# A new written order for the steps of the first kind of layer, on TensorE, ScalarE and VectorE

## The reference

```python
z = rms_norm(x, pre_mix_g) @ w_in            # 3256 columns, cut into 18 parts
o_A = chunk_gla(silu(q) * 64 ** -0.5, k, i, log_f)      # "A", hgrn2: 4 heads of 64
o_B = chunk_gla(q * 32 ** -0.5, k, v, log_gk)           # "B", gla: 4 heads, keys of 32
#   S_t = diag(f_t) S_{t-1} + k_t v_t^T ; o_t = S_t^T q_t
o_C = mla_attention(q_nope, q_rope, k_nope, k_rope, v)  # "C", causal softmax attention
o_D = chunk_gated_delta(qd, kd, vd, beta, log_g)        # "D", gated delta rule, 4 chunks of 64
x = x + rms_norm(concat(o_A, o_B, o_C, o_D) @ w_out, post_mix_g)
# then a gated feed-forward with a causal convolution
```

## Time and profile before

| | before |
|---|---|
| median of 3 runs | 1624.33 us (1623.91 to 1624.46) |
| the profiled execution | 1623.88 us, its span 1621.8 us |
| PE busy | 1538.5 us, 95% of the span |
| DVE busy | 1111.7 us, 69% |
| ACT busy | 811.2 us, 50% |
| mean granted TensorE clock | 0.973 of full |
| mixer of layer 0, first to last matmul | 27.8 to 229.7 us |
| mixer of layer 1 | 443.5 to 647.0 us |

### The profile page before, as it was taken

The page is one execution under the profiler, slowest core; times in us unless marked ns, Lnnn a source line. Parts: engine busy times, 40 slices in busy tenths (PEclk is TensorE's granted clock), DMA queues, the critical chain, the costliest instruction groups (busy, mean ns, idle before and its releaser), DMA issues.

```text
span 1621.8 us, 26707 instructions
## 1 busy us (share of the span) xinstructions
PE 1538.5 (95%) x10572; PEld 1319.4 (81%) x10572; DVE 1111.7 (69%) x1623; ACT 811.2 (50%) x1303; POOL 20.8 (1%) x36
## 2 busy tenths in 40 slices
PE   7998979999999989899999899899999889899998
PEld 7997668888898856788889787788879778788886
DVE  3866677885476666688855887876454798777545
ACT  3533265664435334566544546655355346655334
POOL 0010100000001010000000000000000000000000
PEclk9999889999999989899999899999999999999999
DMA  7431035565553211556563332555545343456552
GB/s 254 152 118 60 24 104 169 167 214 197 168 169 101 80 30 61 183 167 215 188 190 114 113 103 96 175 189 195 198 165 164 104 105 104 130 184 201 199 182 104
DMA packets 185275, 236.62 MB, mean 146 GB/s; under 512 B 24480, under 2 KB 155328, under 8 KB 185024
## 3 DMA queue, kind: packets, MB, share of 16 engines
q1 hardware_dynamic: 182080, 230.18, 44.0%
q0 software_dynamic: 3072, 4.74, 1.1%
HBM read 232.78 MB, written 2.10 MB: 145 GB/s over the span
## 4 chain that ended last, share of the span: by engine, by line
PE 77%; DVE 8%; issue 6%; ACT 3%; DMA 2%; DVEq 2%; ACTq 1%; POOL 0%; SPq 0%; POOLq 0%
PE banks L440 76%; DVE all_ring_rounded L2814 2%; DMA all_ring<-in_w_in 1%; DMA all_ring<-in_w_ple_gate 1%; ACT all_ring_rounded L2632 1%; DVE all_rest L2983 1%; DVE all_work L2918 1%; DVE all_work L2880 1%; DVEq L2917 0%; POOL all_work L2093 0%; PE banks L2299 0%; DVE all_work L2902 0%; DVE all_work L2876 0%; PE banks L955 0%; ACT all_work L351 0%
## 5 line engine op out<-in xcount | busy, mean ns | idle before, releaser
L440 PE MATMUL banks<-all_work_rounded,all_ring_rounded 128*128 128x512 f32 (+2 forms) x4160 | 650.2, 318 | 13.3 <-DVEq L436 10.3
L440 PEld LDWEIGHTS banks<-all_work_rounded,all_ring_rounded 128*128 128x128 f32 (+1 forms) x4160 | 584.8, 190 | 76.6 <-DVEq L436 12.0
L440 PE MATMUL banks<-all_ring_rounded,all_work_rounded 128*128 128x512 f32 (+2 forms) x2304 | 501.8, 378 | 13.5 <-DVE all_ring_rounded L2814 10.4
L440 PEld LDWEIGHTS banks<-all_ring_rounded,all_work_rounded 128*128 128x128 f32 x2304 | 410.1, 192 | 95.9 <-DVE all_ring_rounded L2814 16.1
L2814 DVE TENSOR_TENSOR all_ring_rounded<-all_ring,all_ring_rounded 128x2048 fp32r<-128x2048 f32 x104 | 237.8, 2292 | 119.7 <-ACT all_ring_rounded L2632 117.4
L1641 DVE TENSOR_TENSOR all_ring_rounded<-all_ring,all_ring_rounded 128x2048 fp32r<-128x2048 f32 (+2 forms) x96 | 213.9, 2233 | 72.2 <-ACT all_ring_rounded L1388 70.5
L2632 ACT ACTIVATE all_ring_rounded<-all_ring 128x2048 fp32r<-128x2048 f32 x104 | 198.6, 1912 | 121.2 <-DMA all_ring<-in_w_mlp_down 86.8
L1388 ACT ACTIVATE all_ring_rounded<-all_ring 128x2048 fp32r<-128x2048 f32 (+2 forms) x96 | 177.8, 1859 | 103.3 <-DMA all_ring<-in_w_in 43.4
L440 PE MATMUL banks<-all_work 64*64 64x64 f32 (+8 forms) x2180 | 156.4, 272 | 23.5 <-ACT all_work L2636 9.1
L440 PEld LDWEIGHTS banks<-all_work 64*64 64x64 f32 (+5 forms) x2180 | 114.8, 153 | 58.6 <-issue 24.1
L440 PE MATMUL banks<-all_work,all_ring 128*128 128x128 f32 x704 | 102.1, 289 | 2.4 <-DVEq L409 1.9
(11 more groups left out here) (264 smaller groups left out, 1206.7 us busy)
## 6 DMA issues: line engine op xcount, KB each, us to landing
all_ring<-in_w_in SPq DMA_DIRECT2D x48, 1024.0 KB, 5.4
all_ring<-in_w_mlp_up SPq DMA_DIRECT2D x32, 1024.0 KB, 5.3
all_ring<-in_w_mlp_down SPq DMA_DIRECT2D x32, 1024.0 KB, 4.8
all_ring<-in_ffn_w_gate SPq DMA_DIRECT2D x22, 1024.0 KB, 5.4
all_ring<-in_ffn_w_up SPq DMA_DIRECT2D x22, 1024.0 KB, 5.6
all_ring<-in_ffn_w_down SPq DMA_DIRECT2D x22, 1024.0 KB, 4.9
all_ring<-in_w_out SPq DMA_DIRECT2D x16, 512.0 KB, 4.4
all_ring<-in_w_out SPq DMA_DIRECT2D x8, 1024.0 KB, 5.0
```

The source lines that it names most:

```text
L440: ins = self.nc.tensor.matmul(out, lhsT, rhs, start=start, stop=stop)
```

## The change

Only the three texts of ORDER change, for PE, ACT and DVE. `name:n` means n steps of that part in a row. The set of steps is the same for each engine, but for their order. `panel` and `mix` on PE are empty steps.

```diff
         "PE": in_order("""
-            panel in:3 panel:2 in:3 panel in:8 panel:2 D in:2 panel D panel in:2 A:2 D in panel A D A D A in:3 D panel D
-            A D A panel in panel D A D in panel A D in A D in panel D A D A in A D A in A D:2 panel B D A B D A D mix B
-            D C B D C B D B panel B:3 D:2 B D C D B C B D B C B:2 early D B early C early B early C:2 rest C:2 rest C
-            late mix rest:2 late"""),
+            in:16 D:3 in D in D:2 in A:3 in A D:2 A in A in A D A D A D in A D A in D in A D A in D in D B:2 D A:2 D
+            A:2 D B in D B D B D B C:3 B D B D B D B D B D C B D:2 B C B:2 early B:2 early C:2 early:2 C rest C:2 rest
+            late C rest:2 late panel:16 mix:2"""),
         "ACT": in_order("""
-            panel:4 in panel in:7 panel in:7 D panel in:2 D panel in panel A in D A D in:2 A panel D A:2 D A panel D in
-            D A in D A D in panel:2 A:2 D in D:2 panel D A in:2 A:3 D A D:3 A B mix panel in A D B D:2 B D panel D C B C
-            D B D B:3 D B C B D C B D:2 C B:5 C:2 rest early rest early C rest late rest C late C early C early mix"""),
+            panel:2 in:5 panel:2 in:2 panel in D in:2 D in:2 panel in:2 panel in:2 panel D:2 in:5 A:2 D:2 panel A
+            panel A:2 D:2 A:2 in D:2 A:2 in:2 D:2 A:3 D:2 panel:2 in:2 A:3 panel D:2 in:2 panel D:2 B:2 A:2 D:9 B:2 C
+            B panel:2 B C:2 B:6 C:3 D:2 B:5 C:5 rest:4 early:4 late:2 mix:2"""),
         "DVE": in_order("""
-            in:2 panel:3 in h:2 in:3 panel:2 in panel in:2 D in:7 panel:2 in D in panel in D A:2 D A D:2 in A in A D in
-            A panel D A panel in D in A D panel A D panel in A D:2 in A:2 D:2 in panel A:4 D in panel D B D A D B D:2 B
-            mix B C D C panel B:2 D B:2 D B D:2 B C D B:3 D C B D B C early B:2 mix C early C:4 early late rest:2 C
-            rest:2 late early"""),
+            h in:2 panel:2 in:2 panel h panel in:2 panel in:2 panel in D:2 in:6 D panel:2 D in:2 panel D in:2 A:2 D
+            in:9 D A:2 D panel A:3 D A D panel A:2 D:3 A:4 panel D panel:2 D:3 B A:2 B D:2 B panel D A D B:3 D C:2 B D
+            B D B D B D C D:2 panel mix B:4 C D B:2 C B C mix C:5 early:4 rest:4 late:2"""),
```

## The result

The changed kernel takes 1631.78 us, the median of 5 runs (1629.61 to 1635.21), against 1624.33 before: ratio 1.0052, 95% interval 1.0041 to 1.0063, so 8 us slower. No change to slightly faster was forecast, 1622.2; the time lies just inside the upper end of the range (1632), on the other side of the kernel before. The profiled execution took 1632.31 us around a span of 1630.5, against 1623.88 and 1621.8.

A forecast was written before the change was run, and what follows sets the result against it. TensorE, busy 95% of the span, was taken as the bound, so only waits and clock could change. Gains of 1.9 and 3.6 us in layers 0 and 1, less 2 x 1.7 for clock, left 2.1: 1622.2 us, range 1616 to 1632.

The forecast's parts named there:

- The table loads: ScalarE in each layer's mixer: 13 more loads of 1.28 us, 16.7 us, mostly hidden ahead of waits.
- rival 1: ScalarE: a bare Ln gets the joint set, exposed loads go, 4.2 us faster, 1618.0; chance 0.30 with its neighbour.
- A2's wait: TensorE at A2, start of recurrence A: a wait of 1.5 us for log_f from the Ln chain.
- A15's: TensorE at A15, behind D17: a wait of 1.3 us for the chain from A13 through A14.
- the waits at D24 and D25: After B6: these waits, 1.0 us, go; less 0.2 each at D27 and B13, gain 0.8 us a layer.
- The other waits I find covered: in16 to D17: only A2 adds a wait; v's rows for A come at 105.1, before A6's weighing at 106.2.
- 12.4 us from store to use: Rows of v for B: time from GpSimd's store to B6's weighing, read from layer 1 and used in both layers.
- B6 and D22 at 173.1: Layer 0: rows at 172.0, B6 ends 172.7, D22 173.1 against 173.64 before; gain 0.5 us.
- The clock, 1.7 us in each layer: Half clock behind B6's wait: 1.7 us charged per layer, layer 1 regains 1.7; bounds 0 and half of 11 us.
- a sign of being wrong: Its tests: A2 not waiting, few loads, or half clock from 172 on adding more than 2 us a layer.
- Rival 2: Clock stays low behind v's rows: 3.7 us more per layer, 1629.6; chance 0.20. The forecast's upper clock bound was 5.4.
- The tail, 0.6: Mixer's end: late0 ahead of C10 clears two ScalarE roundings before the next stage's squares; gain 0.6 us a layer.

The follow-up runs named there:

- the joint kernel: Changed kernel with the set holding both Ln and Exp also asked for in D2 and A0; measured 1627.57 us.
- The single edit in the old order: Old order with ScalarE's out3 rounding behind B3, plus TensorE's in27 moved late, behind B2; measured 1628.7 us, against 1621.54 without the in27 move.
- loads and slot mended together: Changed kernel with the joint Ln and Exp set asked for in D2 and A0, and TensorE's in27 right behind in26; measured 1625.87 us.
- in27 early as well: Changed kernel with both the joint Ln and Exp set in D2 and A0 and TensorE's in27 right behind in26; measured 1625.87 us.
- the control: Kernel before the change, with only ScalarE's rounding of out3 (panel14) moved behind B3; measured 1621.54 us.
- in27 early: Changed kernel with only TensorE's in27 moved right behind in26 instead of behind B2; measured 1629.6 us.
- the filling alone: Changed kernel with only D22, C2 and C3 moved ahead of B6 on all engines; measured 1641.6 us.

## Why the prediction failed, point by point

Right were:

- The table loads: 13 more for each mixer, at the places named, 1.28 us each. ScalarE's count grew by 26, and an Exp behind a bare Ln loads again. So rival 1 falls. The price it put on the loads, 4.2 us, is not tested by the joint kernel: the medians differ by 4.2, the ratios by 2.9 us, and the intervals overlap.
- A2's wait, 1.5 forecast and 1.57 found; A15's, 1.3 and 1.27; from D17 to D19 7.8 and 7.84; D19 still waits, behind A15's chain; the waits at D24 and D25 gone (with the new ones there the gain is 0.4 us instead of 0.8).

Wrong were, in order of time:

1. *"The other waits I find covered: v's rows for A ... 105.1 against A6's weighing at 106.2."* The store was at 93.35 instead of 92.7 and landed in 4.7 us, not 2.6, with no load beside it but a packet of the queue `instruction`; the gathers met a 640 KB load of a panel. A6 waited 1.2 us. With it and the 0.5 us of a later start, D17 came at 152.3 instead of 150.4.
2. *12.4 us from store to use, taken as fixed.* This is the step that failed first: a wait of TensorE priced by a transfer time that does not hold in the new order. It was one row, of a place where no load was under way. I followed in27's slot only to ask whether the panel would be in time for ScalarE, and it was; I didn't ask what else its load would meet. The runs showed 15.1, 13.2 and 14.5 us in its place: 0.8 us more for B in layer 0 and 2.1 in layer 1, and 1.2 and 0.4 us of wait for A's rows. The single edit in the old order shows what a load does (2.6 to 4.9 us for the store). In layer 0 it makes the 0.8 (store landed in 3.3 instead of 2.6); in layer 1 the packet of the queue `instruction` is the likely cause of the other 1.4 us, which no run tests.
3. *B6 and D22 at 173.1.* They end at 176.5: 1.9 from D17, 0.8 from the rows, and 0.5 because the weighing itself now runs at half clock, as the wait ends only when the clock has fallen (174.9).
4. *The clock, 1.7 us in each layer against 1.7 given back in layer 1.* This is the second step that failed, by its size: the nearest row was a stretch of 3.4 us, and behind B6 the clock stood at half for 6.8 us in both layers, which is 3.4 us of time at most and not 1.7. The forecast named half clock from 172 on that adds more than 2 us a layer as a sign of being wrong, and it came. The total of the mixers hides it, since the stretch ahead of it, which the forecast didn't price, was 3.3 us shorter in both layers (10.3 for 13.6, 6.9 for 10.2; that layer 1 had one before, from 572.8 to 583.0, the forecast overlooked). In layer 1 there is also one from 461.6 to 465.0, ahead of in6's steps, which no step of the forecast named. So half clock grew by 3.4 to 3.5 us in each mixer, 1.7 us of time: in layer 0 that equals the term of 1.7 by luck, in layer 1 the term was 0. Rival 2's mechanism is what happened in part; it had 5.4 and 3.7. The other half of the mixers' loss is waits. In other executions of kernels with this wait it is more: the joint kernel's 27 and 31 us are over my bound of 11.
5. *The tail, 0.6.* The square does start right behind its bank (233.62), but from the last matmul to the next stage it is 4.30 us against 4.40. The roundings were not what the next stage waited for: the gain is 0.1.

In the sum: forecast per layer were 1.9 us less of waits and tail, and a clock term of 1.7 in layer 0 and 0 in layer 1; found were waits longer by 2.3 and 2.8 and busy time longer by 2.4 and 2.3, of which 1.7 each is clock. Between the forecast (2.1 us less) and the profiled executions (8.7 more) lie 10.8 us. The second step and the first, which carries the same 12.4 us, account for 4.5 of them: a duration that depends on what else moves was read from one row and carried to places with other traffic. The clock within the mixers accounts for 1.7, the tail for 1.0, and the rest is in small terms that were not traced one by one. The chance of 0.20 for rival 2 was too low for the same reason: what spoke against it (TensorE comes late to the rows) supposed rows that come on time.

What stays open: where in time the clock falls in the feed-forward parts, and why it falls at 461.6 us of layer 1: ahead of it TensorE waits 1.8 us for VectorE's drain L425, but it does so for 1.5 in layer 0 and in the kernel before, with no fall. Neither was tried by itself. Nor was a store moved away from the packet of the queue `instruction` alone: A's came right (2.8 us) together with the table loads, when it was issued 2.5 us earlier. That such a packet holds a store up is read from three stores of three kernels, not shown by an edit. The loss is closed to within the measurement by loads and slot mended together, 1.0012 (0.9999 to 1.0025); how much each is worth alone is not.

## What to carry to other kernels

Before you take the time of a small transfer from one row, list what else the new order moves in the same microseconds; a slot given back two steps later is such a load. Work that can fill a wait is worth moving only if it is ready there and not missed where it stood: look at what it waits for in its new place (here an exposed table load) and at what it covered in its old one (here VectorE's split), and mend that in the same edit. And where an order mixes Ln and Exp, ask for the set that holds both at each place where another function may have thrown it out.

## What the runs showed of the hardware

- The clock stays at half long after TensorE is busy again. In the profiled execution of the joint kernel TensorE waited 3.9 and 8.2 us; the granted clock was 0.50 for 27.2 and 30.7 us, of which TensorE was busy 25.1. The changed kernel had waits of 1.7 and 4.6 and half clocks of 6.8 us each. The stretches seen were between 3.4 and 30.7 us long. The Trainium skill, "TensorE: Matmul & The Clock Gate", table "Why this matters for your kernels", tells to leave no gap of some 3 us between bursts; the traces agree for the long waits, within which the clock fell, but it also fell with no gap near that: at 161.2 us of the changed kernel behind waits of 1.3 and 1.1 us, and at 174.9 behind one of 1.7.
- One kernel can give different times from execution to execution: they lie 16 us apart for the joint kernel and 12 with in27 early as well, both with the wait inside B6, and 1.4 for the control.
- A 256 KB store that landed in 2.6 us needed 4.9 with a 1 MB load issued 0.9 us ahead of it, and 3.3 with one issued 2.4 us ahead. Without any load it took 4.4 to 4.9 us in three kernels (the changed one, in27 early, the filling alone), each time with a 16 KB packet of the queue `instruction` that began 1.5 to 1.7 us behind its issue. The first gathers of 128 KB took 4.6 us to land beside a 640 KB load against 2.6. The Trainium skill, "DMA: Bandwidth & Descriptors", section "Queues, rings and completion order", says that each DMA engine takes turns between its queues, a packet at a time; the trace doesn't show such turns: with in27 late no packet of the store's queue moved up to 162.0 us, 3.3 us behind its issue, while 464 of the load's did (alone its first packets moved 1.3 us behind its issue).
- Table loads are cheap where they lie ahead of a wait and dear on the chain that TensorE waits for: 24 cost 12 us in the old order, where three of them stand in ScalarE's queue between A's norm and D18. For 20 of them in the new order the medians give 4 us, within the spread.
